# A hybrid decoder step: seven half-samples of cached values weighted on VectorE, and their tokens summed for four samples at once on TensorE

## What is computed

```python
D_MODEL, SEQ, DEC_BATCH, PAST_LEN, PAGE_SIZE = 2048, 256, 8, 1024, 128
FOX_H, FOX_HD = 4, 128                      # heads, head width

z = x @ w_in                                # (264, 2048) by (2048, 12804)
v_past = cache_v[l][page_table]             # 8 samples x 8 pages x 128 tokens x 512
p = softmax(concatenate([s_past, s_new]))   # 8 samples, 4 heads, 1024 + 1 tokens
o = einsum('bhqk,bkhd->bqhd', p[..., :P], v_past) + einsum('bhqk,bkhd->bqhd', p[..., P:], v)
...
merged = einsum('blkd,blkd->bld', gates, branches @ w_branch)
x = layer_norm(alpha * x + merged @ w_out)
x = layer_norm(alpha * x + (silu(gate) * up) @ w_ffn_down)
```

## Time and profile before

| what | value |
|---|---|
| median of 3 runs | 1729.02 us (1728.69 to 1730.29) |
| the profiled execution: time, and its span | 1729.06 us, 1727.2 us |
| TensorE (PE) busy | 1703.6 us, 99% of the span |
| weight loads of TensorE (PEld) busy | 1647.7 us, 95% |
| VectorE (DVE) busy | 1055.9 us, 61% |
| ScalarE (ACT) busy | 799.2 us, 46% |
| GpSimd (POOL) busy | 61.1 us, 4% |
| granted clock of TensorE, mean | 0.996 |
| stretch 540 to 720 us, in which the 16 units lie | PE 180.0, DVE 95.3, ACT 79.7 us busy, DMA share 0.77, 241 GB/s |

### The profile page before, as it was taken

The page is one execution under the profiler, slowest core; times in us unless marked ns, Lnnn a source line. Parts: engine busy times, 40 slices in busy tenths (PEclk is TensorE's granted clock), DMA queues, the critical chain, the costliest instruction groups (busy, mean ns, idle before and its releaser), DMA issues.

```text
span 1727.2 us, 33354 instructions
## 1 busy us (share of the span) xinstructions
PE 1703.6 (99%) x13830; PEld 1647.7 (95%) x13830; DVE 1055.9 (61%) x1263; ACT 799.2 (46%) x895; POOL 61.1 (4%) x97
## 2 busy tenths in 40 slices
PE   9999999999999999999999999999999999999995
PEld 8999888899999999999999999999999999999995
DVE  7887887756657545455587784444444444454655
ACT  5654544557444444444454564444443444333433
POOL 8200000000010000000000000000000000000000
PEclk9999999999999999999999999999999999999998
DMA  8565567776657977666555556555555555555651
GB/s 262 150 208 159 149 205 243 224 237 212 211 148 237 286 248 233 190 181 183 178 177 185 179 163 195 181 182 181 177 179 180 182 182 181 180 178 170 193 176 73
DMA packets 309127, 329.76 MB, mean 191 GB/s; under 512 B 12175, under 2 KB 289939, under 8 KB 308756
## 3 DMA queue, kind: packets, MB, share of 16 engines
q1 hardware_dynamic: 307612, 326.59, 61.2%
q10 hardware_dynamic: 1400, 1.54, 0.3%
HBM read 322.31 MB, written 5.77 MB: 190 GB/s over the span
## 4 chain that ended last, share of the span: by engine, by line
PE 97%; DVE 1%; DMA 1%; ACT 0%; issue 0%; ACTq 0%; SPq 0%; DVEq 0%
PE ps L747 16%; PE ps L748 15%; PE ps L749 15%; PE ps L1109 15%; PE ps L1110 15%; PE ps L1108 15%; PE ps L837 1%; PE ps L817 1%; PE ps L981 1%; PE ps L796 0%; PE ps L785 0%; PE ps L770 0%; PE ps L763 0%; DMA w_in_ring<-in_w_in 0%; DVE yp L2274 0%
## 5 line engine op out<-in xcount | busy, mean ns | idle before, releaser
L2263 DVE TENSOR_TENSOR w_lo<-w_raw,w_hi 128x1024 fp32r<-128x1024 f32 x264 | 322.7, 1225 | 324.9 <-ACT w_hi L1466 321.8
L1578 DVE TENSOR_TENSOR w_split<-w_in_ring,w_split 128x1024 fp32r<-128x1024 f32 x276 | 338.6, 1230 | 260.8 <-ACT w_split L1170 251.8
L747 PE MATMUL ps<-xh,w_split 128*128 128x264 f32 x1680 | 482.3, 287 | 0.7 <-DVE w_split L1578 0.7
L1466 ACT ACTIVATE w_hi<-w_raw 128x1024 fp32r<-128x1024 f32 x264 | 279.4, 1060 | 438.7 <-PE ps L1110 433.9
L748 PE MATMUL ps<-xl,w_split 128*128 128x264 f32 x1680 | 477.9, 284 | 0.0
L749 PE MATMUL ps<-xh,w_split 128*128 128x264 f32 x1680 | 476.4, 284 | 0.0
L1170 ACT ACTIVATE w_split<-w_in_ring 128x1024 fp32r<-128x1024 f32 x276 | 291.4, 1059 | 362.6 <-DMA w_in_ring<-in_w_in 268.9
L747 PEld LDWEIGHTS ps<-xh,w_split 128*128 128x128 f32 x1680 | 315.9, 188 | 23.8 <-issue 18.1
L1109 PE MATMUL ps<-x1l,w_hi 128*128 128x264 f32 x1152 | 327.6, 284 | 0.0
L1110 PE MATMUL ps<-x1h,w_lo 128*128 128x264 f32 x1152 | 326.8, 284 | 0.0
L1108 PE MATMUL ps<-x1h,w_hi 128*128 128x264 f32 x1152 | 325.8, 283 | 0.0
(11 more groups left out here) (466 smaller groups left out, 2050.0 us busy)
## 6 DMA issues: line engine op xcount, KB each, us to landing
w_in_ring<-in_w_in SPq DMA_DIRECT2D x210, 512.0 KB, 3.7
w_raw<-in_w_ffn_up SPq DMA_DIRECT2D x176, 512.0 KB, 3.5
w_raw<-in_w_ffn_down SPq DMA_DIRECT2D x88, 512.0 KB, 3.4
kv<-in_cache_k SPq DMA_DIRECT2D x64, 258.0 KB, 3.7
w_in_ring<-in_w_branch SPq DMA_DIRECT2D x32, 512.0 KB, 3.5
kv<-in_cache_v SPq DMA_DIRECT2D x64, 256.0 KB, 3.7
w_in_ring<-in_w_out SPq DMA_DIRECT2D x32, 512.0 KB, 3.4
x_t<-in_x SPq DMA_DIRECT2D x8, 264.0 KB, 6.5
```

The source lines that it names most:

```text
L747: nc.tensor.matmul(out, w_split[:, slot, 0, c], right_h[:, k, :], start=first, stop=False)
L1466: A_(w_hi[:, n % RING2, :], raw[:, n % RING2, :], ACT.Copy).then_inc(sem("hi2"), 1)
L1578: V.tensor_tensor(w_split[:, slot, 1, :], w_in_ring[:, slot, 1, :], w_split[:, slot, 0, :], ALU.subtract).then_inc(sem("lo_done"), 1)
L2263: V.tensor_tensor(w_lo[:, n % RING2, :], raw[:, n % RING2, :], w_hi[:, n % RING2, :], ALU.subtract).then_inc(sem("lo2"), 1)
```

## The change

Seven of the eight odd units (`V_SCALED`, all but u = 15) leave TensorE. VectorE takes the four pages of such a unit in two halves, after steps `V_AT[u]` + 3 and + 4: each page's values are multiplied by that page's probability, head by head (128 tokens on the partitions, 128 values of a head), and added up over the four pages in `v_sum`. That is 16 instructions for each unit, 112 in all. TensorE then sums over the 128 tokens with a matrix `heads_of` that holds ones in columns 8h + b: `v_add(0, 4)` for samples 0 to 3 just ahead of unit 8, `v_add(4, 7)` for samples 4 to 6 just ahead of unit 15. The buffer of these seven units is freed by VectorE (`v_scaled`) instead of TensorE (`kv_used`), so SP's wait ahead of the pages of units 3, 5, ... 15 is now for VectorE. GpSimd sets `heads_of` once, behind `ptt`. `v_part` moves to another place in memory.

```diff
+V_SCALED = [1, 3, 5, 7, 9, 11, 13]
...
-    v_part = place("v_part", [P, MIX], F32, at_z + 2 * ZB)
+    v_part = place("v_part", [P, MIX], F32, at_z + 4 * ZB)
+    v_sum = place("v_sum", [P, 4, MIX], F32, at_z + ZB)
+    heads_of = place("heads_of", [P, DEC * (HEADS * DEC + 1)], F32, at_g + 22272)
...
         def load_values(u, first):
-            if first == 0:
+            if first == 0 and u < 2:
                 sp.wait_ge(sem("kv_used"), 16 + u - 1)
-                if u < 2:
-                    sp.wait_ge(sem("lf_taken"), 16 + u - 1)
+                sp.wait_ge(sem("lf_taken"), 16 + u - 1)
+            elif first == 0 and u - 2 in V_SCALED:
+                sp.wait_ge(sem("v_scaled"), V_SCALED.index(u - 2) + 1)
+            elif first == 0:
+                sp.wait_ge(sem("kv_used"), 16 + len([v for v in range(u - 1) if v not in V_SCALED]))
             pages("cache_v", u, first, u // 2, MIX)
...
+        steps.then(pool.memset(heads_of[:, :], 0.0))
+        own = heads_of[:, :].rearrange("p (b m) -> p b m", b=DEC)[:, :, 0:HEADS * DEC]
+        steps.do(pool.memset(own.rearrange("p b (h m) -> p b h m", h=HEADS)[:, :, :, 0], 1.0))
...
+        def v_add(first, end):
+            pe.wait_ge(sem("v_scaled"), end)
+            for b in range(first, end):
+                j = b - first
+                ins = nc.tensor.matmul(PS[32 * j:32 * j + 32, banks("v_unit", 0)[0], :], heads_of[:, 32 * b:32 * b + 32],
+                                       v_sum[:, j, :], start=False, stop=True, tile_position=(0, 32 * j), skip_group_check=True)
+            ins.then_inc(sem("v_added"), 1)
+
         def v_unit(u):
+            if u in V_SCALED:
+                return
             b, half = u // 2, u % 2
+            if u == 8:
+                v_add(0, 4)
+            if u == 15:
+                v_add(4, 7)
...
-        act.wait_ge(sem("kv_used"), 32)
+        act.wait_ge(sem("kv_used"), 32 - len(V_SCALED))
...
+            for u in V_SCALED:
+                if n in (V_AT[u] + 3, V_AT[u] + 4):
+                    scaled_values(u, 2 * (n - V_AT[u] - 3))
...
+        def scaled_values(u, first):
+            b = u // 2
+            if first == 0:
+                dve.wait_ge(sem(f"kv{u % 2}"), 64 * (8 + u // 2 + 1))
+            if u == 1 and first == 0:
+                dve.wait_ge(*told("f_ptt", 1))
+            if b == 4 and first == 0:
+                dve.wait_ge(sem("v_added"), 1)
+            for j in (first, first + 1):
+                for h in range(HEADS):
+                    head = slice(h * P, h * P + P)
+                    out, values = v_sum[:, b % 4, head], kv[:, u % 2, j, head]
+                    at = 32 * (8 * b + 4 + j) + DEC * h + b
+                    if j == 0:
+                        do(V.tensor_scalar(out, values, ptt[:, at:at + 1], None, ALU.mult))
+                    else:
+                        do(V.scalar_tensor_tensor(out, values, ptt[:, at:at + 1], out, ALU.mult, ALU.add))
+                steps.settle()
+            if first:
+                dve.sem_inc(sem("v_scaled"), 1)
```

## The result

| | median | runs |
|---|---|---|
| before | 1728.97 us | 1728.69 to 1730.29, 4 runs |
| with the change | 1740.13 us | 1737.72 to 1740.92, 4 runs |

The ratio is 1.0058, with a 95% interval from 1.0046 to 1.0070. The change costs 11.2 us. The forecast was 1730.5 and its range ended at 1737, so the time lies outside it, on the side that I had given 0.28.

The account below looks back on a forecast made before the run. TensorE, busy 99%, was taken to bound the kernel. 1729.06 - 8.4 (units removed) + 1.7 (added products) + 6.7 (stalls) + 1.5 (later gates) = 1730.5 us; 8-in-10 range 1722.0 to 1737.0.

Parts of the forecast that it names:

- TensorE's loss and gain: On TensorE: seven units removed save 8.4 us, two extra product sets cost 1.7 us, leaving it 6.7 us shorter.
- The halves: VectorE's work on a unit: 2.05 us for the first half, 2.3 for the second; 2.06 if even waits overlapped.
- The gate's length: From one low half through SP's wait, pages and weight load to the third next: 11.4 us.
- The first leads: VectorE's lead over TensorE: 4.45 us at step 162, 1.8 at 165, then -1.0 at 168, stalling TensorE 1.1 us.
- Gate 168 to 171 … Stall 1.8: SP's wait after step 168 delays step 171's weights: lead falls from 0.1 to -1.7 us, TensorE stalls 1.8 us.
- 1.55 us for 174 to 177: SP's wait after step 174 delays step 177's weights: lead falls from 1.2 to -1.45 us, TensorE stalls 1.55 us.
- 2.25 ahead of unit 8: `v_add(0, 4)` waits for unit 7's second half behind `low(180)`: 11.65 us against TensorE's 9.4, a stall of 2.25 us.
- I allow 1.5 us for them (0 to 4): Stalls from the three further gates and their inserted halves after unit 8: 1.5 us, between 0 and 4.
- 3.3 + 1.9 us from `low(177)` to `low(179)`: Low-half spacing on the way to unit 8: 3.3 us plus an estimated 1.9 for one more 512 KB load.
- Rival 2: Gates cost more: with halves of 3.0 us or loads over 0.7 us later, stalls grow, 1735.4 us; chance 0.28.
- Rival 1: Stalls are hidden: 1725.3 us, or 1722.4 if VectorE's lead is never used up; chance 0.24.

Follow-up runs that it names:

- the last experiment: The changed kernel with SP issuing the odd units' pages (from unit 3) two steps later: 1722.71 us, ratio 0.9958.
- e1_vector_alone: The kernel before plus VectorE's 112 instructions on a constant tile, result unused, TensorE keeping all 16 units: 1729.56 us, ratio 1.000.
- e2_no_multiplying: The changed kernel with VectorE's 112 instructions left out and all waits kept: 1723.51 us, ratio 0.9963.
- e6_pages_one_later: The changed kernel with SP issuing the odd units' pages (from unit 3) one step later, behind the next step's weights: 1725.12 us, ratio 0.9970.
- e8_before_gpsimd_queue: The kernel before with the odd units' pages (from unit 3) issued by GpSimd instead of SP, all units on TensorE: 1730.53 us, ratio 0.9999.

## Why the prediction was wrong, point by point

**TensorE's loss and gain: right.** A unit taken away leaves 1.2 us, and the extra set of products costs what was said. TensorE's timeline where `v_add(0, 4)` stands ahead of unit 8:

```profile
633.38 1.06 PE L846 MATMUL ps<-v_sum,heads_of 128*32 128x512 f32 x8
634.26 1.04 PE L864 MATMUL ps<-kv,ptt 128*32 128x512 f32 x8
```

From one to the other it is 0.88 us, for 0.85 forecast. The sum of 6.7 us is confirmed where nothing stalls. TensorE takes 167.3 us from step 158 to step 206 before, and 160.7 with GpSimd's queue. The medians were better by 7.1 us there and by 7.4 in the last experiment, each against its own before.

**The halves: right.** VectorE's timeline has the first half, then later the second:

```profile
581.57 0.87 DVE L1683 TENSOR_SCALAR v_sum<-kv,ptt 128x128 f32<-128x128 f32 x4
582.47 1.14 DVE L1685 SCALAR_TENSOR_TENSOR v_sum<-kv,ptt,v_sum 128x128 f32<-128x128 f32 x4
...
586.47 2.31 DVE L1685 SCALAR_TENSOR_TENSOR v_sum<-kv,ptt,v_sum 128x128 f32<-128x128 f32 x8
```

0.87 and 1.14 with their gaps are 2.05 us (to 583.6), and the second half is 2.31, for 2.05 and 2.3 forecast. The Trainium skill (VectorE: DVE Perf Modes, section on the DRAIN) had a wait between instructions cost nothing, by which a half would be 2.1. The eight with one wait among them took 2.31, and the rows beside it decide. The prediction's working of this bound was also off: with 0.344 us for one alone and 1.13 for four running, the starts are (1.13 - 0.344) / 3 = 0.262 apart, and eight running without a wait come to 0.344 + 7 x 0.262 = 2.18, not 2.06. In the chain above the second four start 1.17 us behind the first (587.64 and 586.47), where four running would take 1.05, so this wait cost 0.12.

**The gate's length: right where it first hurt.** From the end of `low(168)` at 585.33 + 1.23 = 586.56, `low(171)` ended at 598.06, so 11.5 us for 11.4 forecast. The load behind the pages landed in 4.26 us, for 4.4 assumed. The gates to 165, 183, 189 and 195 lasted 11.2 to 11.8 us. Two were longer because their loads came later, the one to 177 (12.1, its load 5.2) and the one to 201 (13.6, its load 5.9).

**The first leads: about right.** The lead at 165 was 1.25 where I had 1.8, and TensorE stalled 2.2 us ahead of 167 and 168 where I had 1.1.

**The step that failed: "Gate 168 to 171 … Stall 1.8".** I reckoned what a late `low(171)` does to TensorE's start of step 171, and took it that the weights were the only thing that came late. The stall came a step earlier, ahead of step 170, and was 5.2 us long. `low(170)` had been ready since 591.51. What was late was ScalarE's evacuation of the gate product, which stands behind `high(171)` in its order and whose banks TensorE wants at step 170. By the weights alone TensorE could have started step 171 at 598.1. With no stall at all it would have come to step 171 at 590.42 + 3.01 + 2.93 = 596.4, so the weights alone cost 1.7 us there, which is the 1.8 of the prediction. By the evacuation it started step 170 at 598.8, and at 2.93 us a step it would have come to 171 at 601.7. This path is 3.6 us longer than the one I followed, and 1.7 + 3.6 are the 5.3 that were measured. I had named what is queued behind SP's wait, and not what is queued behind the instruction that this makes late.

**The second part of the same step: the clock.** I had no term for it. The clock was at its lower level from 597.0 to 603.8, and step 170, which began at 598.8, took 2.3 us more. At step 200 it was 1.6 us more. 4.0 of the 18.0 us are this.

**The later steps.** I had 1.55 us for 174 to 177 and 2.25 ahead of unit 8; neither occurred. The 7.7 us lost at 169 and 170 let VectorE get ahead again, with a lead of 7.3 us at 170 and still 3.9 at 177. "I allow 1.5 us for them (0 to 4)", for the later gates, was too little: they cost 8.2 (steps 189 to 200), 6.5 of it in steps held up by the same evacuation and 1.6 by the clock behind one of them. On the way to unit 8 I had also put 3.3 + 1.9 us from `low(177)` to `low(179)`, the 1.9 an estimate for which no row stood. It was 6.1, and cost nothing. Which gates hurt can be read in the program. The weights behind a wait are those of steps 165, 171, 177, 183, 189, 195 and 201, every six. The gate products are evacuated at ScalarE's steps 171, 176, 181, 186, 191, 196 and 201, every five. The two meet at 171 and at 201, and these are the stalls of 5.3 and 4.0 us (at the start of 170 and 200). At 189 and 195 the evacuation stands two steps and one step behind (191 and 196), and these are the short ones, 1.8 and 0.55. At 177 and 183 it stands ahead (176 and 181) or three steps behind (186), and there is no stall. This is a reading of one trace, and meeting alone is not enough: in the kernel before with the wait, the two meet at 201 as well and TensorE does not stall. The meeting at 201 in the chain that ended last:

```profile
702.07 5.89 DMA w_in_ring<-in_w_in
...
708.95 0.60 ACT gate L1217
...
709.59 0.59 PE ps L759
```

That load took 5.89 us to land, 1.5 longer than the 4.4 that I had allowed for, and so 1.5 of the 4.0 us are the load's lateness. The weights themselves were in time: `low(201)` ended at 710.30, and TensorE without this stall would have come to step 201 at 710.5.

**The sum by its terms.** Forecast 1729.06 - 8.4 + 1.7 + 8.2 of stalls. Measured: 1722.4 + 17.75. The saving stands, and the stalls are mis-sized by 9.6 us, which is how far the forecast was off. Rival 2 had the right sign and for the most part not the right cause. The halves were no longer than I had said, and the load at 171 was no later. Its other condition, loads over 0.7 us later, held at 177, where nothing stalled, and at 201, where it is worth 1.5 us. Rival 1 is what the kernel does once SP's wait is out of the weights' way.

**What stays open.** That waits lower the clock was argued from their order in time and not tried by itself. It fell during the wait of 5.2 us and behind that of 3.8 here, during the one of 4.7 in the kernel before with the wait, and within 1.2 us behind shorter ones too: 2.4 us in the kernel with the pages one step later, and 2.6 with the evacuation ahead (granted clock 0.93 from 660 to 680 us). With the evacuation ahead it stayed at 1.00 from 590 to 620 us, where the longest wait was 1.8. That kernel's steps are 14.1 us longer in this stage than with GpSimd's queue, and 1.5 of them are the step behind its fall.

## What to carry to other kernels

When a wait is put on an in-order queue, list everything behind it, then everything behind each instruction that this makes late, on every engine, up to the one that is full; an evacuation behind a late load can be wanted sooner than the load. Where two periodic jobs share an engine, write their steps side by side, since the stalls fall where they meet. If the transfer behind the wait has slack, move its issue behind the urgent ones before changing anything else: here two steps later were worth 17.4 us by the medians.

## What the runs showed of the hardware

- In a wait of TensorE of 5.2 us the granted clock fell to half, 1.8 us before the wait ended, and came back 5.0 us after it (0.51 from 597 to 604 us). Behind one of 3.8 us it was at half for 3.4 us (0.58 from 709 to 713). They lost a further 2.3 and 1.6 us. A wait of 2.4 us in the kernel with the pages one step later was followed by 3.4 us at half clock and a loss of 1.5. The short waits at steps 166 and 167 (1.8 us in two) show no such fall.
- A fall doesn't follow every such wait. All ten traces have one of 2.0 to 2.1 us that ends between 925 and 944 us, where TensorE's next long run of products begins. The clock fell behind it in four of them (`e1_vector_alone` 0.86 from 930 to 934 us and 0.81 from 934 to 940, and likewise in `e2_no_multiplying`, `e6_pages_one_later` and `e8_before_gpsimd_queue`) and in the other six it did not.
- Busy time hides this: TensorE's sum was 1702.4 us after, and 1697.1 with GpSimd's queue, for the same 13788 instructions. The 5.3 us between them are loss that counts as work, 4.0 of it in the two steps at the lower clock.
- GpSimd as a second queue for 28 pages of 256 KB cost no time (1730.53 us against 1730.12 before). The pages landed in 4.4 us at the median there, for 4.0 by SP in the same kernel.
